# Sixteen consecutive pairs of experts summed by products, and row sums moved forward, in a hybrid decoder layer

## The chip, the cores and the metric

One Trainium2 chip, one core. The metric is the device time of one execution in microseconds (us), lower is better. The kernel is written by hand for each engine, with semaphores between them: TensorE (PE) for products, VectorE (DVE), ScalarE (ACT), GpSimd (POOL), and SyncE (SP), which issues the loads of weights.

## The reference, cut to what matters

One layer for 264 tokens (256 of a prompt, 8 samples), width 1024, all in float32. RWKV-7 time mixing and a convolution module are merged and projected, then comes the channel mixer, in which the change lies: 64 experts of width 256, of which each token takes 8 (out of 4 of 8 groups), and one shared expert.

```python
gate = jnp.sum(jax.nn.one_hot(eidx, N_EXPERTS) * wsel[..., None], axis=1)    # 8 of 64 per token
def expert_block(args):
    xb, gb = args
    h = silu(einsum('td,edf->tef', xb, w_gate)) * einsum('td,edf->tef', xb, w_up)
    h = h * gb[..., None]
    return einsum('tef,efd->td', h, w_down)
y = h + routed + shared        # then the final RMSNorm
```

Each expert has three matrices of 1 MB (w_gate, w_up, w_down), so the stage reads 192 MB of weights, in the order of the experts.

## The kernel before, in words

The first half of the run (to about 490 us) is the mixing part and the router. The change does not touch it.

In the experts' stage the experts are worked in 32 pairs, at places 0 to 31. Each expert has 64 slots, a pair fills the 128 rows of the array: two experts' matmuls run as halves (64 x 512). The weights stand in a ring of five slots (`NSLOT`), which SP refills when TensorE has finished with a slot (gate and up after `h_mm`, down after `yx_mm`), so weights are loaded about two and a half pairs ahead.

For a pair at place q TensorE does in this order, in the loop over q in `moe_pe`: `index(q+3)` (3 matmuls of one column that turn a one-hot tile into a list of token rows), `gate_up(q)` in two halves of 16 matmuls, between them `turn_hidden(q-1)` (2 transposes, L626), then `down(q-1)` (16 matmuls), and `turn(q+1)` (8 transposes of the next pair's token rows, L595). The token rows are gathered from `xg` by POOL (L1159). ACT makes the sigmoid, copies the turned tiles and stores half of the down product (`ye_act`); DVE multiplies the hidden tile (`hidden`, L981 and L982) and stores the other half (`take`, L990, `ye_dve`).

The pair's result `ye` (128 slots x 1024) comes to the tokens' sum `xrow` by one of two ways:

- **Stored pairs.** Four steps later POOL writes the rows that hold a token to `yrows` in DRAM with an indirect DMA (L1203). When all stored pairs are written, 24 gathers (`early_rows`, L1173: 3 tiles of tokens times their 8 experts, in order of tiles 0, 2, 1; tile 2 has 8 rows) bring rows back into a ring of five tiles (`NEB`), and DVE adds each one, weighted, with `add_early` (L1056). Rows of experts that were not stored are left out by the bounds check.
- **Product pairs** (`late(q)`). DVE makes a tile of gates (`late_gates`, L1017 to L1025) and TensorE turns it (`turn_gates`, 3 transposes, L660). Two places later TensorE multiplies it with `ye` (`combine(q)`, 4 small matmuls for the samples and 4 of 128 x 512) and DVE adds the product to `xrow` (`add_late`, L1035 and L1039). Nothing goes to DRAM.

Which pair is what is set by the tuple `LATE` (L337). Experts are renumbered over the places so that the stored pairs hold the lowest numbers (`PAIR`, `ROW_LIMIT`). `SUMS_FROM` and `SUMS` (L344) say how many of the 24 row sums are done by which place. In `pair(q)` on DVE half of a place's sums, rounded down, stand ahead of `hidden(q)`, the rest behind it, and `take(q-1)` behind those. At place 31 all stand ahead. On POOL, step i first fetches the token rows of pair i, then stores pair i-4, then issues the gathers of `rows_by(i)` to `rows_by(i+1)`: none before step `LAST_STORED + 4`, where it waits for all stores to land and issues five; after that as many in step i as the sums of place i-3. A gather waits for the sum that frees its tile. Step i starts after turn(i-2), which stands at the end of place i-3.

Of the kernel before, what the change touches and what calls it, by code (L numbers as in the profile page):

```python
# [111 lines left out]
def layer_step(nc, A, out, stop=9):  # L112

    ctx = ExitStack()
    with ctx:
# [218 lines left out]
        rowl = E.take(3, 8).bitcast(U32)  # L334
        E8 = x2T.rearrange("p k n -> p (k n)")[:, 0:8 * NE].rearrange("p (a e) -> p a e", a=8)
        NPAIR = NE // 2
        LATE = (14, 16, 18, 20, 24, 25, 26, 27, 28, 29, 30, 31)  # L337
        NLATE = len(LATE)
        FIRST = NPAIR - NLATE
        late = lambda q: q in LATE  # L340
        nlate = lambda q: sum(p < q for p in LATE)
        PAIR = [FIRST + nlate(q) if late(q) else q - nlate(q) for q in range(NPAIR)]
        LAST_STORED = max(q for q in range(NPAIR) if not late(q))
        SUMS_FROM, SUMS = 26, (0, 4, 8, 12, 16, 20, 24)  # L344
        sums_by = lambda q: SUMS[max(0, min(q - SUMS_FROM, len(SUMS) - 1))]
        NEB = 5
        xeT = [E.take(KT, 2 * SLOTS) for _ in range(2)]
# [1850 lines left out]
```

How the kernel before makes its waits and increments, by code:

```python
            def link(ins, name):  # L261
                note(ins, name)
                eng.wait_ge(S[name], cnt[name])
# [6 lines left out]
        def wait(eng, name, k):  # L270
            if k > 0:
                eng.wait_ge(S[name], k)
# [11 lines left out]
        def z_wait_free(eng, n):  # L284
            if n >= 2:
                kind = z_kind(n - 2)
                eng.wait_ge(S[f'z_free_{kind}'], sum(z_kind(m) == kind for m in range(n - 1)))
# [144 lines left out]
        def moe_sp(sp):  # L433
            for part, n in enumerate(('ws_gate', 'ws_up')):
                load_item(sp, part, SHARED_SLOT, A[n][0])
            for e in range(3):
                for part in range(3):
                    load_item(sp, part, e, expert_w(part, e))
            load_item(sp, 2, 3, expert_w(2, 3))
            sp.wait_ge(S['h2_ready'], 8)
            load_item(sp, 0, 4, expert_w(0, 4))
            sp.wait_ge(S['x2_ready'], 3)
            sp.dma_start(grow, A['normf_g'].rearrange("(a d) -> a d", a=1).partition_broadcast(128)) \
              .then_inc(S['grow_in'], 16)
            sp.dma_start(xg[0:NP, :].rearrange("(t p) d -> p t d", p=128), x2p[:, 0:2, :]).then_inc(S['x2_out'], 16)
            sp.dma_start(xg[NP:NT, :], x2p[0:NS, 2, :]).then_inc(S['x2_out'], 16)
            load_item(sp, 1, 4, expert_w(1, 4))
            sp.dma_start(wsd, A['ws_down'][0].rearrange("(j p) d -> p j d", p=128)).then_inc(S['wsd_in'], 16)
            sp.wait_ge(S['mk_ready'], 1)
            load_item(sp, 2, 4, expert_w(2, 4))
            sp.wait_ge(S['shg_mm'], 4)
```

## Time and profile before

| | us |
|---|---|
| median of 3 runs | 1061.78 |
| lowest, highest | 1061.06, 1062.14 |
| the profiled execution | 1062.62 |
| its span, first to last instruction | 1060.8 |
| TensorE busy | 955.1 (90%) |
| DVE busy | 526.3 (50%) |
| POOL busy | 330.0 (31%) |
| ACT busy | 233.7 (22%) |

The page divides the span into 40 slices of 26.5 us. TensorE's granted clock is given in tenths of full speed; a value of 1.00 is 2.4 GHz over the whole stretch, lower values are a mix with 1.2 GHz. In a timeline a number in brackets is the engine's idle time ahead of the row, and behind the arrow stands what ended it. A wait for several semaphores is put down to the one that came last. DMA's share is the mean busy share of 16 DMA engines.

### The profile page before, as it was taken

The numbers are of one execution on the slowest core, as the hardware profiler recorded it, in microseconds if no ns is written. First come the engines' busy times: TensorE is split into PE (matmuls) and PEld (weight loads), VectorE is DVE, ScalarE is ACT, GpSimd is POOL, SyncE is SP. The second block draws the span as 40 slices with busy tenths as digits, with TensorE's granted clock in tenths as the row PEclk, the third lists the DMA queues.
The fourth block names the chain that finished last, engine by engine and source line by source line (L and its number), as shares of the span: only waits on it lengthen the run. The fifth ranks groups of instructions, "written<-read, shape, count | busy, mean of one in ns | idle before, by whom it ended". The sixth has DMA issues, their size and how long they took to land.

```text
span 1060.8 us, 18129 instructions
## 1 busy us (share of the span) xinstructions
PE 955.1 (90%) x7399; PEld 572.7 (54%) x7399; DVE 526.3 (50%) x1053; ACT 233.7 (22%) x486; POOL 330.0 (31%) x363
## 2 busy tenths in 40 slices
PE   5999999999999988699998898879899998998995
PEld 4878877877787786348443333333333433333331
DVE  2158958875985778766232311111222321264665
ACT  3241134114312511433111111121111111111113
POOL 0049907951992498000011111010110101222310
PEclk9999999999999999899998999989999999999998
DMA  8635243525424265198799999999999999999961
GB/s 232 175 124 195 91 147 127 191 81 172 160 96 137 72 216 222 25 390 324 269 408 422 420 416 414 417 407 408 405 398 410 397 417 416 413 414 393 345 226 42
DMA packets 87502, 292.67 MB, mean 276 GB/s; under 512 B 17058, under 2 KB 48356, under 8 KB 62567
## 3 DMA queue, kind: packets, MB, share of 16 engines
q1 hardware_dynamic: 72647, 254.03, 62.2%
q0 software_dynamic: 14768, 37.43, 9.3%
q8 instruction: 61, 1.00, 0.4%
q14 instruction: 26, 0.21, 0.1%
HBM read 275.48 MB, written 33.16 MB: 291 GB/s over the span
## 4 chain that ended last, share of the span: by engine, by line
PE 64%; DMA 19%; DVE 7%; ACT 3%; SPq 3%; issue 2%; POOL 0%; DVEq 0%; POOLq 0%
PE bank L1358 62%; DMA big<-in_w_up 17%; ACT big L1655 3%; DMA big<-yrows,big 2%; DMA big<-in_w_in 1%; DVE big L1945 1%; SPq L400 1%; PE bank L595 1%; PE bank L626 1%; SPq L1311 1%; DVE big L1998 1%; DVE big L2002 0%; ACT L1655 0%; DVE big L1153 0%; SPq L1265 0%
## 5 line engine op out<-in xcount | busy, mean ns | idle before, releaser
L1358 PE MATMUL bank<-big 64*64 64x64 f32 (+8 forms) x6914 | 892.0, 358 | 84.8 <-DMA big<-in_w_up 35.5
L1358 PEld LDWEIGHTS bank<-big 64*64 64x64 f32 (+4 forms) x6914 | 517.5, 149 | 410.5 <-issue 316.3
L1655 ACT ACTIVATE big<-bank 128x512 f32<-128x512 f32 (+7 forms) x286 | 122.7, 452 | 663.6 <-PE bank L1358 388.7
L1159 POOL DMA_INDIRECT big<-xg,big x32 | 33.4, 1044 | 475.7 <-PE bank L595 374.3
L2149 POOL TENSOR_SCALAR big<-big 128x256 f32<-128x256 f32 x120 | 132.6, 1105 | 1.7
L981 DVE TENSOR_TENSOR big<-big,bank 128x256 f32<-128x256 f32 x32 | 13.5, 421 | 209.8 <-ACT big L1655 209.8
L2161 POOL TENSOR_TENSOR big<-big 128x256 f32<-128x256 f32 x120 | 94.2, 785 | 0.3
L1945 DVE SCALAR_TENSOR_TENSOR big<-big 128x256 f32<-128x256 f32 x120 | 79.6, 663 | 4.1
L1655 ACT ACTIVATE big<-big 128x272 f32<-128x272 f32 (+9 forms) x108 | 49.9, 505 | 43.6 <-DVE big L1880 11.3
L990 DVE COPY big<-bank 128x512 f32<-128x512 f32 x32 | 22.1, 689 | 57.2 <-PE bank L1358 57.2
L1655 ACT ACTIVATE big<-bank,big 128x272 f32<-128x272 f32 (+2 forms) x53 | 23.8, 475 | 111.9 <-PE bank L1358 111.9
L2145 POOL TENSOR_SCALAR big<-big 128x256 f32<-128x256 f32 x4 | 2.2, 550 | 148.3 <-DVE big L1923 148.3
L595 PEld LDWEIGHTS bank<-big 128*128 128x128 f32 x256 | 27.4, 141 | 25.2 <-issue 25.2
L1039 DVE TENSOR_TENSOR big<-big,bank 128x512 f32<-128x512 f32 x48 | 33.0, 689 | 14.4 <-PE bank L1358 14.4
L1655 ACT ACT_TABLE_LOAD x30 | 38.5, 1283 | 3.2 <-DVE big L899 2.0
L1173 POOL DMA_INDIRECT big<-yrows,big x24 | 26.0, 1081 | 37.1 <-DVE big L1056 19.2
L1862 DVE SCALAR_TENSOR_TENSOR big<-bank,big 128x272 f32<-128x272 f32 x26 | 12.9, 496 | 45.4 <-ACT big L1655 45.4
L595 PE MATMUL bank<-big 128*128 128x128 f32 x256 | 35.0, 280 | 0.0
L1056 DVE SCALAR_TENSOR_TENSOR big<-big 128x1024 f32<-128x1024 f32 (+1 forms) x24 | 30.7, 1278 | 7.3 <-DMA big<-yrows,big 6.2
L1025 DVE COPY big<-bank 128x264 f32<-128x264 f32 x12 | 5.2, 433 | 42.5 <-PE bank L660 42.5
L626 PEld LDWEIGHTS bank<-big 128*128 128x128 f32 x64 | 10.1, 205 | 26.0 <-issue 26.0
L1203 POOL DMA_INDIRECT yrows<-big x20 | 21.4, 1070 | 6.1 <-issue 6.1
(164 smaller groups left out, 441.3 us busy)
## 6 DMA issues: line engine op xcount, KB each, us to landing
big<-in_w_gate SPq DMA_DIRECT2D x64, 1024.0 KB, 15.5
big<-in_w_up SPq DMA_DIRECT2D x64, 1024.0 KB, 21.0
big<-in_w_down SPq DMA_DIRECT2D x64, 1024.0 KB, 14.1
big<-in_w_in SPq DMA_DIRECT2D x29, 1024.0 KB, 5.2
yrows<-big POOLq DMA_DIRECT2D x32, 512.0 KB, 3.3
big<-in_w_out SPq DMA_DIRECT2D x2, 2048.0 KB, 14.8
big<-in_state_wkv SPq DMA_DIRECT2D x32, 64.0 KB, 2.3
out_wkv_s<-big SPq DMA_DIRECT2D x32, 64.0 KB, 3.7
```

The source lines that it names most:

```text
L595: ins = nc.tensor.transpose(ps_x[h][:, 128 * (k % 4):128 * (k % 4) + 128], xe[q % NXE][:, 128 * k:128 * k + 128], ident)
L990: note(v.tensor_copy(ye[q % NYE][:, 512:1024], ps_y[1][:, :]), 'ye_dve')
L1039: note(v.tensor_tensor(x, x, comb_bank(q, n), AD), 'cb_sum')
L1056: note(v.scalar_tensor_tensor(out=xrow[0:r, t, :], in0=early[k % NEB][0:r, :], scalar=gate8a[0:r, t, j:j + 1], in1=xrow[0:r, t, :], op0=M, ...
L1159: pool.indirect_dma_start(out=x[0:n, :], out_offset=None, in_=xg, in_offset=bass.IndirectOffsetOnAxis(ap=idxu[0:n, col:col + 1], axis=0), ...
L1173: pool.indirect_dma_start(out=early[k % NEB][0:r, :], out_offset=None, in_=yrows[0:PASS, :], in_offset=bass.IndirectOffsetOnAxis(ap=rowu[0 ...
L1203: pool.indirect_dma_start(out=yrows[0:PASS, :], out_offset=bass.IndirectOffsetOnAxis(ap=rowsu[:, c:c + 1], axis=0), in_=ye[q % NYE], in_of ...
L1358: return nc.tensor.matmul(out_, lhsT=lhsT, rhs=rhs, start=start, stop=stop)
L1655: return nc.scalar.activation(out_, in_, f, **kw)
L1945: note(v.scalar_tensor_tensor(out=acc, in0=u, scalar=cw, in1=acc, op0=M, op1=AD), 'tap')
L2149: note(gp.tensor_scalar(TP[:, w % 3, :], u, cw, None, ALU.mult), 'tapm')
L2161: note(gp.tensor_tensor(acc, acc, TP[:, w % 3, :], ALU.add), 'tapm')
```

## The change

Sixteen pairs, at places 16 to 31, are product pairs in place of twelve (14, 16, 18, 20 and 24 to 31). With that the places 14 and 15 are both stored, and 17, 19, 21, 22, 23 are no longer. The last stored pair is 15 in place of 23, so POOL's wait for the stores and its first five gathers stand in step 19 in place of 27. The row sums are spread three to a place over places 19 to 26, in place of four to a place over 26 to 31. `PAIR` becomes the identity, `ROW_LIMIT` goes from 2560 to 2048 rows.

```diff
-        LATE = (14, 16, 18, 20, 24, 25, 26, 27, 28, 29, 30, 31)
+        LATE = tuple(range(16, 32))
...
-        SUMS_FROM, SUMS = 26, (0, 4, 8, 12, 16, 20, 24)
+        SUMS_FROM, SUMS = 19, (0, 3, 6, 9, 12, 15, 18, 21, 24)
```

On TensorE, place 19 before: index of 22 (bank0, 128x1), the two halves of the gate and up products (bank4) around turn_hidden (bank5), down (bank6, bank7) and turn (bank1, bank2).

```order
L1358 MATMUL bank0<-big 128x1 x3
L1358 MATMUL bank4<-big 64x512 x8
L626 MATMUL bank5<-big 128x128 x2
L1358 MATMUL bank4<-big 64x512 x8
L1358 MATMUL bank6<-big 64x512 x4
L1358 MATMUL bank7<-big 64x512 x4
L595 MATMUL bank1<-big 128x128 x4
L595 MATMUL bank2<-big 128x128 x4
```

The same place in the changed kernel, up to the down products.

```order
L1358 MATMUL bank0<-big 8x256 x4
L1358 MATMUL bank1<-big 128x512
L1358 MATMUL bank2<-big 128x512
L1358 MATMUL bank1<-big 128x512
L1358 MATMUL bank2<-big 128x512
L1358 MATMUL bank0<-big 128x1 x3
L1358 MATMUL bank4<-big 64x512 x8
L626 MATMUL bank5<-big 128x128 x2
L660 MATMUL bank0<-big 128x128 x2
L660 MATMUL bank0<-big 128x8
L1358 MATMUL bank4<-big 64x512 x8
```

The combine of pair 17 (the first five rows) and the gate transposes of pair 19 (L660) have come in. A row of x8 stands for 16 matmuls of the trace where each is issued in two parts.

On POOL, the end of the stage before: from the store of pair 23 (the second row) on. L1159 fetches token rows, L1203 stores, L1173 is a gather for a row sum.

```order
L1159 DMA big<-xg,big 128x1024
L1203 DMA yrows<-big 4096x1024
L1173 DMA big<-yrows,big 128x1024 x5
L1159 DMA big<-xg,big 128x1024 x2
L1173 DMA big<-yrows,big 128x1024 x3
L1173 DMA big<-yrows,big 8x1024
L1159 DMA big<-xg,big 128x1024
L1173 DMA big<-yrows,big 8x1024 x4
L1159 DMA big<-xg,big 128x1024
L1173 DMA big<-yrows,big 8x1024 x3
L1173 DMA big<-yrows,big 128x1024 x8
```

And of the changed kernel, from the store of pair 15 in step 19 on, up to step 28.

```order
L1203 DMA yrows<-big 4096x1024
L1173 DMA big<-yrows,big 128x1024 x5
L1159 DMA big<-xg,big 128x1024 x3
L1173 DMA big<-yrows,big 128x1024 x3
L1159 DMA big<-xg,big 128x1024
L1173 DMA big<-yrows,big 8x1024 x3
L1159 DMA big<-xg,big 128x1024
L1173 DMA big<-yrows,big 8x1024 x3
L1159 DMA big<-xg,big 128x1024
L1173 DMA big<-yrows,big 8x1024 x2
L1173 DMA big<-yrows,big 128x1024
L1159 DMA big<-xg,big 128x1024
```

The gathers have moved eight steps forward, and a step now issues three of them, each group behind the fetch of a pair's token rows.

## Rows read from the trace of the kernel before

**Rows 1.** The page's 40 slices: busy tenths, clock, DMA and GB/s.

```profile
PE   5999999999999988699998898879899998998995
PEclk9999999999999999899998999989999999999998
DMA  8635243525424265198799999999999999999961
GB/s 232 175 124 195 91 147 127 191 81 172 160 96 137 72 216 222 25 390 324 269 408 422 420 416 414 417 407 408 405 398 410 397 417 416 413 414 393 345 226 42
```

**Rows 2.** Chain that ended last, by time: start us, us, what.

```profile
692.95 19.17 DMA big<-in_w_up
...
888.96 20.43 DMA big<-in_w_up
...
946.91 16.62 DMA big<-yrows,big
...
1003.51 8.03 PE bank L1358 x32
```

**Rows 3.** Timeline of TensorE, places 14 to 28: start us, us, operation, idle before.

```profile
729.03 5.35 PE L1358 MATMUL bank<-big 128*64 128x512 f32 x16 [2.03 <-DMA big<-in_w_up]
...
734.65 0.54 PE L660 MATMUL bank<-big 128*128 128x128 f32 x3
...
742.14 1.09 PE L595 MATMUL bank<-big 128*128 128x128 f32 x8
...
745.86 5.35 PE L1358 MATMUL bank<-big 128*64 128x512 f32 x16 [1.98 <-DMA big<-in_w_up]
...
811.63 5.35 PE L1358 MATMUL bank<-big 128*64 128x512 f32 x16 [1.60 <-DMA big<-in_w_up]
...
943.13 8.67 PE L1358 MATMUL bank<-big 128*8 128x256 f32 x38 [0.94 <-ACT big L1655]
```

**Rows 4.** Windows: places 16-17, 17, 18-23, 24-27, 27, 28, 29.

```profile
core 0: us, PE busy (x) PEld busy (x) DVE busy (x) ACT busy (x) POOL busy (x), PEclk, DMA share, GB/s
758.59:789.82 31.23, 30.31 (x150) 12.30 (x148) 9.47 (x22) 4.86 (x10) 3.03 (x3) 1.00 0.98 399
776.95:789.82 12.87, 12.78 (x67) 5.24 (x65) 2.44 (x7) 2.43 (x5) 2.02 (x2) 1.00 0.96 383
789.82:887.54 97.72, 92.24 (x441) 37.47 (x439) 26.93 (x63) 14.58 (x30) 9.09 (x9) 0.98 1.00 410
887.54:959.56 72.02, 64.75 (x303) 26.60 (x301) 29.21 (x56) 9.72 (x20) 14.92 (x15) 0.95 1.01 415
941.10:959.56 18.46, 17.52 (x86) 7.06 (x84) 9.89 (x18) 2.43 (x5) 4.89 (x5) 1.00 1.02 413
959.56:983.66 24.10, 18.95 (x85) 7.51 (x83) 13.42 (x20) 2.43 (x5) 5.33 (x5) 0.93 0.92 362
983.66:1001.48 17.82, 16.89 (x80) 6.18 (x78) 11.00 (x16) 2.43 (x5) 7.50 (x8) 1.00 0.95 355
```

**Rows 5.** Timeline of DVE, places 26 to 31, row sums and takes.

```profile
941.58 0.68 DVE L990 COPY big<-bank 128x512 f32<-128x512 f32 x1
...
955.98 1.28 DVE L1056 SCALAR_TENSOR_TENSOR big<-big 128x1024 f32<-128x1024 f32 x1 [1.71 <-DMA big<-yrows,big]
...
963.55 1.28 DVE L1056 SCALAR_TENSOR_TENSOR big<-big 128x1024 f32<-128x1024 f32 x1 [2.45 <-DMA big<-yrows,big]
964.76 0.68 DVE L990 COPY big<-bank 128x512 f32<-128x512 f32 x1
...
1035.91 0.68 DVE L990 COPY big<-bank 128x512 f32<-128x512 f32 x1
1037.81 0.42 DVE L981 TENSOR_TENSOR big<-big,bank 128x256 f32<-128x256 f32 x1 [1.22 <-ACT big L1655]
```

**Rows 6.** Timeline of POOL: first gather of its 27th step, next fetch, next gathers.

```profile
922.80 1.02 POOL L1173 DMA_INDIRECT big<-yrows,big  x1 [12.12 <-DMA yrows<-big]
...
929.30 0.99 POOL L1159 DMA_INDIRECT big<-xg,big  x1 [0.30 <-issue]
...
944.32 0.99 POOL L1173 DMA_INDIRECT big<-yrows,big  x1 [0.30 <-issue]
```

## The prediction, made before the changed kernel had run

> **What bounds the kernel now.** I read first the page's 40 slices, to find the stage that the change touches: from about 500 us on, the experts' stage, DMA is busy nine tenths or more and moves 400 GB/s and more until slice 37 [rows 1]. The page's TensorE digit is also 8 or 9 there, so the averages don't say which of the two sets the pace. The chain of waits does, by place in the order of pairs: where a pair is stored the chain goes through the landing of w_up, and it goes through TensorE's matmuls alone in the last pairs; between them stands one piece of 16.62 us on a gather from yrows [rows 2].
>
> The TensorE timeline gives the period of each pair, if one takes the start of turn (L595 x8) as a pair's end. Two things are to be seen in it [rows 3]. At places 14, 15 and 19 TensorE waits 1.6 to 2.0 us for w_up, and then its first 16 matmuls of gate and up take 5.35 us. At a product pair the x38 row (combine, index and the same 16) starts after 0.94 us of idle on ACT's release and needs 8.67 us, with no wait for DMA behind it.
>
> The windows turn that into prices [rows 4]. Place 17, a pair without combine that didn't wait, took 12.87 us. Place 27, with index, combine and gate transposes, took 18.46 us, of which TensorE was busy 17.52 us at a granted clock of 1.00 (2.4 GHz). Place 29, which has no index, took 17.82 us. So a combine with the gate transposes and the idle around it costs TensorE 5.6 us. DMA's pace lies between: from the w_up-bound start at 745.86 (place 15) to that at 811.63 (place 19) are 65.77 us for four pairs, 16.44 us a pair [rows 3]. A stored pair is under the DMA's pace by 3.6 us, a product pair is over it by 2.0 us. **Before, the two kinds alternate from 14 to 20 and a product pair's excess is paid out of its neighbour's slack. That is what the change takes away.**
>
> **The change part by part.** The order of instructions says it does what its table says: at place 19 TensorE now has a combine and gate transposes, and POOL starts its gathers four places after store 15 rather than after store 23. Everything below is measured against the profiled execution (span 1060.8 us, its own time 1062.62 us; the median of the runs, 1061.78 us, is 0.84 us less).
>
> Places 0 to 15: nothing. The experts' order there differs only at 14 and 15. Place 14 loses its three gate transposes (0.54 us) behind a wait for w_up of 1.98 us at place 15 [rows 3], which covers them; that cover would not have to be there for a loss, only for the absence of a gain. Place 14 gains a store. 264 tokens times 8 rows of 4 KB are 2112 rows over 32 pairs, so 66 rows or 0.27 MB a pair: 0.66 us at the 410 GB/s of the stage [rows 4], and it is issued in place 16.
>
> Places 16 and 17: they lose the combine of 14, since 14 and 15 are now stored, so nothing covers the wait for w_up. Before they took 31.23 us at clock 1.00 without a DMA wait [rows 4]. Now the DMA's pace decides: place 17's gate products start two periods after 745.86, at 778.7, and from such a start to the next turn are 13.11 us (729.03 to 742.14, with gate transposes) [rows 3]. End of 17 at 791.8 instead of 789.82: **+2.0 us**. Bounds: 0 if the weights are ahead, +3.3 with both extra stores in front of them.
>
> Places 18 to 23: six pairs with index, combine and gate transposes, 6 x 18.46 = 110.8 us. Before these six took 97.72 us, three of them without a combine [rows 4]: **+13.0 us**. Is TensorE really the bound there? From 18 to 26 the DMA must move 9 x (6 weights of 1.05 MB and 0.27 MB of token rows) = 59.0 MB, and the 24 gathers, half of the 2112 rows, 4.3 MB: 63.3 MB, at 410 GB/s 154 us against 9 x 18.46 = 166 us. It has 12 us over, and the sums' load is not even: three full gathers together are 1.6 MB, 3.8 us, less than the 2 us a pair that have been gathered up by then plus the ring's lead. The sum has no DMA wait in it.
>
> A rule of the Trainium skill speaks against this kernel at this point: DMA: Bandwidth & Descriptors, Specifications, gives a core about 358 GB/s of HBM. By that the 63.3 MB would need 177 us, an estimate from that page, and the sum would be 11 us more. This trace differs: 410 and 415 GB/s over 97.72 and 72.02 us [rows 4], and the measurement decides.
>
> Places 24 to 27: 4 x 18.46 = 73.84 us against 72.02 us; the old stretch had two DMA waits but also one pair without combine [rows 4]: **+1.8 us**.
>
> Place 28: it took 24.10 us, 5.64 us more than its work [rows 4]. The vector engine's rows say why: the row sums (L1056) of the place ahead waited again and again for a gather, the last ended at 964.8, and only then came take (L990), on which the combine of 26, at the head of place 28, waits [rows 5]. The gathers were issued from 944.32 on, three us into the pair that needed them, and three of its four sums fed on them [rows 6]. The change makes the sums three a pair, so only the last of the three feeds on a gather issued at the end of the pair before; the other two have been out a pair longer. Place 28 itself has no sums left. 24.10 becomes 18.46: **-5.6 us**. Could the stall only move? In place 27 the first gather, issued at 944.32, let its sum start at 955.98, 14.9 us into the pair; two sums behind the hidden products are harmless if they end by 18.9 us into the pair, as they did in place 26, where take ran from 941.58 and the x38 row still started on ACT's release [rows 3, 5]. The third sum starts at about 17.6, so 2.7 us are left at the three places (20, 25, 26) where its gather is a large one. I take nothing for it; the ends are 0 and the whole 5.6 us again.
>
> Place 29 to the end: the four row sums of place 31 go, but take of 30 there waited for nothing that they held: hidden of 31 started at 1037.81 on ACT's release, 1.22 us after take had ended, so they lay in cover [rows 5]. **0 us.** The vector engine's own load is no bound: 9.89 to 13.42 us in pairs of 18.46 and more [rows 4]. POOL at its 19th step waits for store 15 and then issues five gathers. Before that was 12.12 us of idle and 6.4 us of issue, and the next token gather stood behind it [rows 6]; its pair is turned more than a pair later, so it costs nothing. If that cover failed, turn would wait.
>
> Sum: 2.0 + 13.0 + 1.8 - 5.6 = **+11.2 us**, 1073.8 us for a run like the profiled one and **1073.0 us** beside the median. The clock is in these rows: all prices of product pairs are at 1.00. The x16 row's 5.35 us after each DMA wait would vanish with the waits, and this is inside the 18.46.
>
> **The rivals.** (A) The gather stall stays, at one of places 20, 25, 26, or at several: the DMA queue stays full and the third gather lands later than 17.6 us into its pair. For it: one landed 16.62 us after issue [rows 2]. Against it: that was the last of four with full rows; its price is 2 to 5.6 us, 1075 to 1078.6 us, and more at two places.
>
> (B) The DMA doesn't recover. Place 29 moved only 355 GB/s with a busy share of 0.95 [rows 4]. If mixing products and loads held the DMA to that, 63.3 MB need 178 us, 12 us over TensorE's 166: about 1085 us. Against it: place 27 did the same work at 413 GB/s.
>
> (C) Faster: the DMA is the bound all the way and its bytes decide. Four stores and an eighth of the gathers' rows go, 2 x 264 rows of 4 KB = 2.2 MB, 5.3 us at 410 GB/s, and the stall of 5.6 us too: 1062.62 - 10.9 = 1051.7 us. It decides if a product pair can run below 16.4 us. The row of place 27 with 17.52 us of TensorE's busy time at full clock speaks against it.
>
> (D) No change: places 16 to 23 lose, but the end gains the same, because the waits of 24, 25 and 28 and the x16 rows at low clock held more than I count: 1060 to 1064 us. The prices above leave no room for it.
>
> **How the numbers follow.** A measurement of this kernel can tell about 0.2%, 2.1 us, from no change. My forecast, +8 to +14 us, has 0.78; A 0.11; B 0.05; C 0.03; D 0.03. The range takes in the forecast's bounds below (no loss at 16 and 17, some waits shorter: -3 us) and A's one stall above: 1070 to 1079 us. B, C and D and the upper part of A are left out. Faster 0.03, same 0.03, slower 0.94.
>
> **What would show it.** In the profile after: turn-to-turn periods of 18.46 us from place 18 to 28, no wait for w_up behind place 17, and the GB/s digits down to about 355 to 390 from slice 30 on. Place 16 starts its gate products on w_up, near 762. Row sums start near place 19 and none is left after place 26; DVE waits for yrows come to under 3 us in all. The chain runs from place 18 to the end in TensorE. I am wrong if waits for w_up come back after 18 (B), if take ends late behind a sum (A), or if product pairs run below 18 us (C).

## The result, and the profile after

The changed kernel takes 1076.52 us (median of 4 runs, 1073.83 to 1077.90), the kernel before 1061.42 us in the same comparison. The ratio is 1.0144 with a 95% interval of 1.012 to 1.0167: slower by 1.4%, some 15 us. The forecast was 1073.0 us, in a range of 1070 to 1079.

The profiled execution took 1077.1 us, its span is 1074.7 us, 13.9 us more than before. The page of the changed kernel, its slices:

```profile
PE   5999999999999987799989889888899999999995
PEclk9999999999999999899999899989899999999997
DMA  8645253425524275296899999999999999998911
GB/s 229 174 128 196 80 169 120 168 81 169 186 103 124 67 252 177 93 421 235 335 419 419 404 420 417 415 414 410 386 412 412 416 363 379 382 399 343 380 63 42
```

Beside [rows 1], TensorE's digit is 9 from slice 30 to 39 without a break, and the GB/s fall to 343 to 399 in slices 33 to 38; before, slices 33 to 36 had 413 to 417. The queue is no longer what the last part of the stage waits for.

The windows, cut at the starts of turn (the transposes of the next pair's token rows, L595): places 16 and 17, 18 to 23, 24 to 27, 28, 29 and 30, and the end from turn(31) on.

```profile
core 0: us, PE busy (x) PEld busy (x) DVE busy (x) ACT busy (x) POOL busy (x), PEclk, DMA share, GB/s
757.10:789.80 32.70, 29.17 (x136) 12.11 (x135) 7.91 (x20) 4.86 (x10) 4.08 (x4) 0.90 0.97 387
789.80:900.46 110.66, 105.15 (x500) 42.35 (x499) 59.58 (x105) 14.57 (x30) 22.32 (x23) 1.00 0.99 400
900.46:974.31 73.85, 70.11 (x335) 28.25 (x333) 39.30 (x70) 9.72 (x20) 10.89 (x11) 1.00 0.95 384
974.31:992.77 18.46, 17.52 (x86) 7.05 (x84) 6.56 (x14) 2.43 (x5) 0.98 (x1) 1.00 0.89 356
992.77:1028.40 35.63, 33.76 (x156) 12.35 (x155) 12.34 (x22) 4.86 (x10) 0.99 (x1) 1.00 0.77 307
1028.40:1074.70 46.30, 32.42 (x129) 11.49 (x127) 19.10 (x32) 11.06 (x22) 0.00 (x0) 0.86 0.13 47
```

The stage can be added up against [rows 4]:

| stretch | before, us | after, us | difference | forecast |
|---|---|---|---|---|
| up to the end of place 15 | 758.59 | 757.10 | -1.5 | 0 |
| places 16 and 17 | 31.23 | 32.70 | +1.5 | +2.0 |
| 18 to 23 | 97.72 | 110.66 | +12.9 | +13.0 |
| 24 to 27 | 72.02 | 73.85 | +1.8 | +1.8 |
| 28 | 24.10 | 18.46 | -5.6 | -5.6 |
| 29 and 30 | 35.64 | 35.63 | 0 | 0 |
| from turn(31) to the end | 41.50 | 46.30 | +4.8 | 0 |
| sum | 1060.8 | 1074.7 | +13.9 | +11.2 |

(35.64 is 1019.30, the start of turn(31) before, less 983.66, the end of place 28.) From places 16 and 17 down to 29 and 30 the table is within 0.5 us of the forecast. The first line is not, and the last is off by 4.8 us. The timeline of TensorE in the changed kernel, first at places 16, 17 and 18, then at the end:

```profile
762.15 6.52 PE L1358 MATMUL bank<-big 128*64 128x512 f32 x16 [3.31 <-DMA big<-in_w_up]
...
778.39 3.65 PE L1358 MATMUL bank<-big 128*64 128x512 f32 x16 [0.22 <-DMA big<-in_w_up]
...
791.72 8.68 PE L1358 MATMUL bank<-big 128*8 128x256 f32 x38 [0.83 <-ACT big L1655]
...
1051.54 3.65 PE L1358 MATMUL bank<-big 128*64 128x512 f32 x16 [0.47 <-ACT big L1655]
1058.95 7.14 PE L1358 MATMUL bank<-big 128*8 128x256 f32 x16 [3.76 <-issue]
```

The waits for w_up end with place 17, as forecast. From there to place 30 TensorE has no gap but the 0.9 us ahead of each combine. The last row is the combine of pair 31. The kernel before has this row at the same point:

```profile
1047.18 4.26 PE L1358 MATMUL bank<-big 128*8 128x256 f32 x16 [1.10 <-DVE big L990]
```

Before, it starts 0.35 us after the vector engine's copy and needs 4.26 us. Now it starts 3.0 us after that copy, released by nothing that the profile's waits show, and needs 7.14 us. Over these matmuls the granted clock is 0.59, most of them at half the clock, as their window shows:

```profile
1058.90:1066.20 7.30, 7.14 (x16) 2.48 (x16) 3.49 (x6) 3.25 (x7) 0.00 (x0) 0.59 0.00 0
```

The chain of waits of the changed kernel has the stall as a piece of its own:

```profile
1051.54 3.68 PE bank L1358 x16
1055.21 0.02 issue
1055.24 0.70 DVE big L990
1055.94 3.02 issue
1058.95 4.77 PE bank L1358 x12
1063.72 0.02 issue
1063.75 0.69 DVE big L1039
```

What stands between the two matmul rows in TensorE's program is a branch: `with pe.If(count > SLOTS)`, the overflow pass for experts with more than 64 tokens, which isn't taken with these inputs, so TensorE jumps over its code to `combine(NPAIR - 1)`. The experiments begin there.

### The profile page after: what moved, and what is told of

Its sections match the earlier page's. It is cut to its first block, busy times and chain, and to the rows that moved or that the text cites. A ratio compares the mean times of both kernels' runs of the same rounds, so it can differ in the third digit from the quotient of the medians.

```text
span 1074.7 us, 18349 instructions
## 1 busy us (share of the span) xinstructions
PE 972.3 (90%) x7475; PEld 577.7 (54%) x7475; DVE 543.8 (51%) x1085; ACT 233.7 (22%) x486; POOL 323.0 (30%) x359
## 3 DMA queue, kind: packets, MB, share of 16 engines
q8 instruction: 62, 1.02, 0.4%
## 4 chain that ended last, share of the span: by engine, by line
PE 70%; DMA 14%; DVE 7%; ACT 4%; SPq 3%; issue 2%; DVEq 0%
PE bank L1358 67%; DMA big<-in_w_up 13%; ACT big L1655 3%; DMA big<-in_w_in 1%; DVE big L1945 1%; PE bank L595 1%; PE bank L626 1%; SPq L400 1%; SPq L1311 1%; DVE big L1998 1%; PE bank L660 0%; DVE big L2002 0%; ACT L1655 0%; DVE big L1153 0%; SPq L1265 0%
## 5 line engine op out<-in xcount | busy, mean ns | idle before, releaser
L1358 PE MATMUL bank<-big 64*64 64x64 f32 (+10 forms) x6978 | 907.1, 359 | 82.7 <-DMA big<-in_w_up 31.3
L1358 PEld LDWEIGHTS bank<-big 64*64 64x64 f32 (+4 forms) x6978 | 521.1, 149 | 419.8 <-issue 320.2
L1159 POOL DMA_INDIRECT big<-xg,big x32 | 33.3, 1042 | 476.7 <-PE bank L595 399.6
L1039 DVE TENSOR_TENSOR big<-big,bank 128x512 f32<-128x512 f32 x64 | 44.0, 689 | 19.4 <-PE bank L1358 19.4
L595 PEld LDWEIGHTS bank<-big 128*128 128x128 f32 x256 | 27.4, 141 | 25.2 <-issue 25.2
L1862 DVE SCALAR_TENSOR_TENSOR big<-bank,big 128x272 f32<-128x272 f32 x26 | 12.9, 496 | 45.8 <-ACT big L1655 45.8
L595 PE MATMUL bank<-big 128*128 128x128 f32 x256 | 35.0, 280 | 0.0
L1173 POOL DMA_INDIRECT big<-yrows,big x24 | 23.2, 968 | 19.3 <-DMA yrows<-big 12.3
L1035 DVE TENSOR_TENSOR big<-big,bank 104x256 f32<-104x256 f32 x16 | 6.7, 421 | 30.2 <-PE bank L1358 30.2
```

The source lines that it names most:

```text
L595: ins = nc.tensor.transpose(ps_x[h][:, 128 * (k % 4):128 * (k % 4) + 128], xe[q % NXE][:, 128 * k:128 * k + 128], ident)
L1039: note(v.tensor_tensor(x, x, comb_bank(q, n), AD), 'cb_sum')
L1159: pool.indirect_dma_start(out=x[0:n, :], out_offset=None, in_=xg, in_offset=bass.IndirectOffsetOnAxis(ap=idxu[0:n, col:col + 1], axis=0), ...
L1173: pool.indirect_dma_start(out=early[k % NEB][0:r, :], out_offset=None, in_=yrows[0:PASS, :], in_offset=bass.IndirectOffsetOnAxis(ap=rowu[0 ...
L1358: return nc.tensor.matmul(out_, lhsT=lhsT, rhs=rhs, start=start, stop=stop)
```

## The experiments

All times are medians against the kernel before on the same chip; "the end" is the stretch from turn(31) on, 41.50 us in the kernel before.

**1 and 2. The branch taken out, of both kernels.** These two leave out TensorE's part of the overflow pass.

```diff
-            with pe.If(count > SLOTS):
-                for c in range(1, MAXPASS):
...
             combine(NPAIR - 1)
```

> The changed kernel with TensorE's branch around the overflow pass taken out (the branch and what it skips; it isn't executed with these inputs, so the pass is left out on TensorE alone). Theory 1 (code behind a taken branch): the 3.76 us in which TensorE stood before the combine of pair 31, released by nothing, and the low clock after it (7.14 us for 16 matmuls instead of 4.26) are the branch. Both go: the span from turn(31) to the end falls from 46.3 to 41 us or less, the time by 4.5 to 6 us. Theory 2 (the stretch depends on who is late there, the row sums having gone from place 31): the 46.3 us stay within 0.5 us.

Measured: 1072.19 us, 4.3 us below the changed kernel (5.4 between the profiled executions), ratio to the kernel before 1.0119 (1.0083 to 1.0155). This interval overlaps with the changed kernel's (1.012 to 1.0167), so the times alone don't settle it; the place of the difference in the trace does. The timeline of TensorE in this kernel, and the window of the end:

```profile
1051.49 3.65 PE L1324 MATMUL bank<-big 128*64 128x512 f32 x16 [0.47 <-ACT big L1621]
1056.25 4.26 PE L1324 MATMUL bank<-big 128*8 128x256 f32 x16 [1.10 <-DVE big L956]
```

```profile
1028.36:1069.80 41.44, 29.54 (x129) 10.58 (x127) 19.11 (x32) 11.07 (x22) 0.00 (x0) 0.93 0.14 52
```

The end is 41.44 us again. The stall and the low clock behind it are both gone, and the 18.46 us of each place are as they were (turn(19) at 808.14, turn(29) at 992.74 us).

> The same cut in the kernel before. Theory 1: the 1.10 us idle before the combine of 31 become about 0.3 to 0.4 after the vector engine's copy, or about 0.8 less; time lower by 0 to 1.5 us, much less than for the changed kernel. Theory 2: the same, no difference. If this falls by as much as the changed kernel does, the branch costs both the same and the 4.8 us are something else.

Measured: 1061.78 us, ratio 1.0009 (0.9989 to 1.0029), with 1.10 us of idle and 4.26 us of combine as with the branch. The expectation had room for a small gain; there is none. So the branch costs nothing in the profile of the kernel before and 4.8 us in that of the changed kernel. Its mere presence isn't the cause.

**3 to 5. The code moved.** Matmuls of one column made twice, at places 3 to 15, where TensorE waits for weights. They write the same values again and make the program longer: 13 lists of three matmuls, 78 matmul records. The diff is that of pad_before.

```diff
+                if 6 <= q <= 18:
+                    lists(2 * SLOTS, q % NIX, OH[q % 2])
                 note(lists(2 * SLOTS, q % NIX, OH[q % 2]), 'idx_mm')
```

> The kernel before with 13 lists of three one-column matmuls made twice (places 3 to 15), 78 matmul records more, about as many as the four combines of the change add (76), all in places where TensorE waits for the DMA. Theory 1 in its narrow form (what counts is how far the branch stands in TensorE's program): the end from turn(31) on goes from 41.5 to about 46.3 us, the time up by 4 to 5 us, with the rest unchanged. Theory 2, or a stall of the branch that doesn't hang on the position: the end stays at 41.5 us, time within 1 us of before.

Measured: 1064.28 us, ratio 1.0042 (1.0022 to 1.0062), 3.7 us over the kernel before where 4 to 5 were expected. The timeline of TensorE:

```profile
1042.41 0.61 PE L1360 MATMUL bank<-big 128*8 128x256 f32 x6 [1.10 <-DVE big L992]
1044.50 5.76 PE L1360 MATMUL bank<-big 128*8 128x256 f32 x10 [1.48 <-issue]
```

The kernel before now has a stall too, at another point: six matmul records of the combine run, then TensorE stands for 1.48 us with nothing to release it, and the other ten take 5.76 us. From the start of the combine to the end of the span are 17.2 us (1042.41 to 1059.6) instead of 13.6, and the end is 45.1 us, where 46.3 were expected.

The same on the changed kernel, with 7 and with 14 lists:

> The changed kernel with 7 lists of three one-column matmuls made twice at places 3 to 15 (42 matmul records), in the shadow of the waits for w_up there. Theory 1 (the stall at the branch hangs on where the code behind it stands): the 3.76 us of idle before the combine of 31 change, to 1.10 us or to a piece that cuts the combine, while the 18.46 us of places 18 to 28 stay. If they stay at 3.0 to 3.8 us with a low clock behind them, position within a hundred instructions isn't what counts.

> The same with 14 lists (84 records). Theory 1: again another stall than the changed kernel's, and the three together (0, 42, 84 records more) differ by 2 us or more in the end from turn(31) on. Rival: all three within 1 us of 46.3 us.

Measured, one execution each: 1074.66 and 1073.40 us, and the row of the combine is in both what it was before the change. With 14 lists:

```profile
1057.98 4.26 PE L1361 MATMUL bank<-big 128*8 128x256 f32 x16 [1.10 <-DVE big L993]
```

The end is 41.4 us in both. One execution each says little in time, since the changed kernel's own go from 1073.83 to 1077.90 us, but the row is plain: 42 matmul records more in the program remove the stall. All kernels with the branch, by the length of TensorE's program:

| kernel | matmul records more than before | idle at the combine of 31, us | its matmuls, us |
|---|---|---|---|
| before, sums_before, sums2_before | 0 | 1.10 | 4.25 to 4.26 |
| alt13 | 19 | 1.10 | 4.26 |
| alt14, run14, alt14_s3 | 38 | 1.10 to 1.17 | 4.26 |
| changed kernel | 76 | 3.76 | 7.14 |
| late_only | 76 | 3.56 | 5.95 |
| pad_before | 78 | 1.10, then 1.48 | 0.61 and 5.76 |
| pad_after7 | 118 | 1.10 | 4.26 |
| pad_after14 | 160 | 1.10 | 4.26 |

The alt kernels, run14, the sums kernels and late_only are described further down. The stall comes at 76 to 78 records more and at no other length tried, also in late_only, which has the changed kernel's program on TensorE and other row sums. Its cause is the length of the code ahead, not what the engines did. The Trainium skill has a mechanism for it (Runtime: NRT & Kernel Launch, Instruction fetch mechanics): a sequencer streams its instructions in blocks of 16 KiB, one after another, and a taken branch whose target isn't in the window forces a fetch of the target's block.

The traces show such fetches. The page lists an instruction queue with 61 packets and 1.00 MB before, 16.4 KB each; without TensorE's branch and the code that it skips there are 59, and 60 in place of the changed kernel's 62. The DMA view of 8 us around the combine, in 40 slices of 0.2 us, where 82 GB/s in one slice are one such packet: the changed kernel from 1052, the kernel before from 1043, pad_before from 1038.

```profile
GB/s 0 0 0 82 0 0 0 0 0 0 0 0 0 0 0 0 0 0 0 0 82 0 41 0 0 0 0 0 0 0 0 0 0 0 0 0 0 0 0 0
```

```profile
GB/s 0 0 82 0 0 0 0 0 0 0 0 0 0 0 0 0 0 0 0 82 0 0 0 0 0 0 0 0 0 0 0 0 0 0 0 0 0 0 0 0
```

```profile
GB/s 0 0 0 82 0 0 0 0 0 0 0 0 0 0 0 0 0 0 0 0 82 0 0 0 0 0 0 0 0 0 0 0 0 0 0 0 0 0 0 0
```

Each has two packets 3.4 us apart (the 41 belongs to another, smaller queue). In the changed kernel the second starts near 1056.1 and TensorE goes on at 1058.95, 2.8 us later. In pad_before it starts near 1042.1 and TensorE goes on in mid-combine at 1044.50, 2.4 us later; in late_only near 1062.1 and at 1064.45, 2.3 us later. In the kernel before it starts near 1046.9, and the combine runs from 1047.18 without a break. This fits one reading: the first packet brings the branch's target, the second the code behind it, and TensorE stands only where it runs off the first block before the second is in. Which instructions a packet holds no trace shows, and no padded kernel was run without the branch.

**6 and 7. Product pairs: how many, or where?** Both have fourteen of them and move the same bytes, with the same row sums (3, 3, 4, 5, 5, 4 a place). New against the kernel before are 12 and 22 in alt14, 17 and 19 in run14.

```diff
+        LATE = (12, 14, 16, 18, 20, 22, 24, 25, 26, 27, 28, 29, 30, 31)        # alt14
+        LATE = (14, 16, 17, 18, 19, 20, 24, 25, 26, 27, 28, 29, 30, 31)        # run14
+        SUMS_FROM, SUMS = 26, (0, 3, 6, 10, 15, 20, 24)
```

> Fourteen product pairs, the two new ones (12 and 22) with a stored pair on either side, and row sums at 3, 3, 4, 5, 5, 4 from place 26 on. Theory P (a product pair costs only where its neighbour is one too: 18.46 us of TensorE against a DMA pace of 16.4, and 12.87 for a stored pair): the two cost nothing, and 0.54 MB of stores and as much of gathers go, 2.6 us. So 0 to 3 us faster than the kernel before with the same row sums (sums2_before). Rival N (each product pair costs its 5 us of TensorE, wherever it stands): 4 to 10 us slower than sums2_before.

> Also fourteen product pairs and the same row sums as alt14, with the same number of stores and gathered rows, but the new ones are 17 and 19, so that 16 to 20 are five in a row. Theory P: places 17 and 19 take 18.46 us each instead of 12.9 and 16.1; of these 8 us some come back at 21 to 23, where TensorE waited 3 to 4 us for w_up. So 3 to 7 us slower than alt14 and sums2_before. Rival N: the same as alt14 within 1 us.

Measured: alt14 1054.99 us, ratio 0.9953 (0.9937 to 0.9968); run14 1065.94 us, ratio 1.0040 (1.0023 to 1.0058). Where the two new pairs stand makes 11 us, more than the 3 to 7 expected. Theory P holds, with sizes larger than expected, and rival N (no difference) falls. Against sums2_before (1058.88 us) alt14 is 3.9 us faster and run14 7.1 us slower. Places 16 to 20 and 21 to 23 of run14:

```profile
757.98:845.17 87.19, 83.25 (x401) 33.96 (x399) 32.05 (x70) 12.15 (x25) 6.02 (x6) 1.00 0.96 394
845.17:894.22 49.05, 47.09 (x227) 18.71 (x225) 13.58 (x31) 7.29 (x15) 3.99 (x4) 1.00 0.90 361
```

In and behind the run of five the DMA falls back to 394 and 361 GB/s. A fair comparison must hold the same work. A pair's combine stands two places behind it, so the stretch is places 14 to 26, in which each kernel has seven combines; run14, then alt14:

```profile
723.80:947.18 223.38, 205.96 (x973) 83.74 (x971) 69.89 (x156) 31.59 (x65) 24.09 (x24) 0.97 0.97 395
```

```profile
723.57:936.20 212.63, 201.28 (x970) 82.26 (x968) 68.45 (x153) 31.59 (x65) 24.24 (x24) 0.99 1.00 407
```

Both start it at the same time, and run14 ends it 11.0 us later, of which 10.8 are its own. alt14 takes 16.4 us a place, the DMA's pace of the prediction, with the queue full all the way. run14 lets the queue fall back in places 16 to 23 and has to wait for weights afterwards: place 25 starts its products after 3.64 us of idle on w_up and takes 19.6 us, and the DMA is at 417 GB/s over places 25 and 26. What TensorE won back at places 23 and 24 (12.87 and 13.87 us) it paid again at 25 and 26 (19.56 and 19.53); the expectation had seen only the first half of this. The spans differ by 12.5 us; the other 1.5 are in the end.

**8 to 10. The row sums.**

> The changed kernel's sixteen product pairs with the old row sums (26 to 31, four a place). The stores have landed long before; the first five gathers are issued at step 19, the others from place 26 on, one pair before use, as in the kernel before. Theory S with the DMA's load as its cause: from place 18 on TensorE is the bound and the queue is no longer full, so gathers land in under 10 us and place 28 has no stall; the time is that of the changed kernel within 1.5 us (1074 to 1078, if the branch costs the same). Theory S with the freshness alone as its cause: the stall of place 28 is back, 3 to 5.6 us over the changed kernel.

Measured: 1080.85 us, ratio 1.0194 (1.0167 to 1.0220), 4.3 us over the changed kernel's median, which is from another comparison; 4.7 between the profiled spans. Places 27 and 28:

```profile
954.84:973.30 18.46, 17.52 (x85) 7.06 (x84) 9.90 (x18) 2.43 (x5) 4.90 (x5) 1.00 0.94 377
973.30:998.38 25.08, 18.97 (x85) 7.54 (x83) 13.42 (x20) 2.43 (x5) 5.16 (x5) 0.86 0.77 306
```

and the vector engine in them:

```profile
969.55 1.29 DVE L1056 SCALAR_TENSOR_TENSOR big<-big 128x1024 f32<-128x1024 f32 x1 [1.53 <-DMA big<-yrows,big]
...
974.55 1.29 DVE L1056 SCALAR_TENSOR_TENSOR big<-big 128x1024 f32<-128x1024 f32 x1 [2.93 <-DMA big<-yrows,big]
...
978.26 1.29 DVE L1056 SCALAR_TENSOR_TENSOR big<-big 128x1024 f32<-128x1024 f32 x1 [2.42 <-DMA big<-yrows,big]
979.47 0.68 DVE L990 COPY big<-bank 128x512 f32<-128x512 f32 x1
```

The stall is back in full, 6.6 us instead of 5.6, though the DMA now runs at 377 GB/s in place 27 (busy share 0.94) instead of 413 (1.02). The three fresh gathers, issued at 958.40, 959.70 and 961.00, let their sums start 11.2, 14.9 and 17.3 us later; in the kernel before it was 11.7, 14.2 and 16.6 us. What counts is that a sum's gather is issued in the place that needs it; a queue that is a tenth less loaded didn't make it faster. How a gather fares beside an idle queue was not run. Without its new row sums the change would have cost 4 to 5 us more.

The other side, the kernel before with gentler row sums:

```diff
-        SUMS_FROM, SUMS = 26, (0, 4, 8, 12, 16, 20, 24)
+        SUMS_FROM, SUMS = 26, (0, 3, 6, 10, 14, 19, 24)        # sums_before
+        SUMS_FROM, SUMS = 26, (0, 3, 6, 10, 15, 20, 24)        # sums2_before
```

> The kernel before with its row sums at 3, 3, 4, 4, 5, 5 a place from 26 on, instead of six times 4. Theory S (the stall of 5.6 us in place 28 is the fresh gathers: three of four sums of place 27 feed on gathers issued in that place): the sums of place 27 feed on the first five gathers, place 28 takes 18.5 us instead of 24.1, and the time falls by 4 to 6 us, to about 1056. Rival (the queue is full and the wait moves to place 28 or 29, or to the five sums of place 31): a wait of 2 us or more for yrows there, and the time falls by less than 3 us.

> The kernel before, row sums at 3, 3, 4, 5, 5, 4 a place. The earlier spread with five sums ahead in place 31 lost 1.9 us there (take was late by 1 us, combine after it by as much). Theory S: with four in place 31 the end from turn(31) on is 41.5 us again, place 28 stays near 18.5 to 19.5, and the time is 4 to 6 us under the kernel before. Rival: the five fresh gathers of place 30 are late and take 1 to 3 us back.

Measured: 1057.86 us, ratio 0.9987 (0.9970 to 1.0004), and 1058.88 us, ratio 0.9984 (0.9969 to 0.9998). The stall is gone in both (place 28 takes 19.5 and 18.5 us), but the gain is about half of the 4 to 6 us that I expected, and in sums_before under the 3 us that the expectation gave to its rival. Part is given back where five sums stand in one place, as sums2_before's timeline of TensorE shows at the head of places 30 and 31:

```profile
998.52 8.03 PE L1358 MATMUL bank<-big 128*8 128x256 f32 x32 [1.78 <-DVE big L990]
...
1017.25 8.03 PE L1358 MATMUL bank<-big 128*8 128x256 f32 x32 [1.85 <-DVE big L990]
```

The idle time is 0.94 with four sums; each place with five costs 0.85 to 0.9 us. In sums_before the five of place 30 and the five ahead of take in place 31 made the end 43.4 us (1011.27 to 1054.7), 1.9 us more. In place 26, the first with row sums, TensorE takes 18.46 us as before, so their effect starts at turn(27). From there on the profiles are 2.7 and 3.9 us shorter (117.0 and 115.8 us against 119.7); the medians fell by 2.7 and 2.4. The profiled spans fell by 6.1 and 4.1 us, but what goes beyond lies ahead of that point and is scatter.

**11 and 12. Attempts at better.**

> alt14 with row sums at 3, 4, 4, 4, 5, 4. Five sums in a place made TensorE wait 0.85 us more for take at the head of places 30 and 31; here only one place has five. Theory S: 0.8 us less there, but place 27 has two fresh gathers of four sums instead of one of three, whose second may come 1 us late: the time within 1 us of alt14. Rival (freshness decides): place 28 gets a stall of 2 us or more.

Measured: 1056.34 us, ratio 0.9942 (0.9922 to 0.9962), not to be told from alt14. One of the two waits of 1.8 us for take is left, and places 27 and 28 are 18.46 us each: two fresh gathers of four sums are still harmless.

> One more stored pair in the alternation (25, with 24 a product pair), so the run of product pairs is 26 to 31; the first gathers can't be issued before step 29 and 24 row sums must fit in places 28 to 31 (5, 6, 7, 6). Theory P alone: place 25 and 26 take the DMA's pace instead of 18.46, 3 to 4 us less than alt14. Theory S: six sums a place with a ring of five tiles wait for gathers of 10 us and more, 4 to 12 us lost at places 29 to 31. I expect S to win: 2 to 8 us slower than alt14.

Measured: 1069.90 us, ratio 1.0080 (1.0054 to 1.0107), 15 us over alt14, nearly twice what I had expected at most. TensorE waits five times for take at places 29 to 31, 17.4 us in all (the last of them the 1.10 us that every kernel without the stall has); the three longest:

```profile
976.52 9.68 PE L1358 MATMUL bank<-big 128*8 128x256 f32 x32 [4.28 <-DVE big L990]
...
1001.18 9.45 PE L1358 MATMUL bank<-big 128*8 128x256 f32 x32 [6.13 <-DVE big L990]
...
1022.97 8.03 PE L1358 MATMUL bank<-big 128*8 128x256 f32 x32 [3.49 <-DVE big L990]
```

Six and seven sums a place don't fit beside the pair's own work with a ring of five tiles.

alt14 beats both kernels: 0.47% (0.32 to 0.63%) under the kernel before. It has more product pairs than that and fewer than the changed one, and none of the new ones next to another.

## Why the prediction was right, and where it wasn't

- **The bound changes at place 18, and a product pair is 18.46 us.** Right to 0.1 us over ten places: 110.66 for six, 73.85 for four. Run14 against alt14 shows the mechanism apart from the number of pairs. The working says that 24 to 27 had one pair without combine before; there were two, 24 and 25, since a combine stands two places behind its pair. The 72.02 us are measured, so the sum isn't touched.
- **Places 16 and 17.** Forecast +2.0, measured +1.5. The wait for w_up at place 16 came as said, at 762.15 us. At place 17 it was only 0.22 us, at 778.39 us where 778.7 was worked out. Place 17 ended at 789.80 us, not at 791.8: the gain ahead of place 16 hides in the +1.5.
- **Nothing ahead of place 16.** The profile has -1.5 us there. The places are the same but for gate transposes and one store, and noif_after reached the same point at 756.11 us. So did noif_before, with the old order, at 755.75 us. I take it for scatter: of 25 executions of the kernel before in one comparison the times go from 1054.9 to 1063.1 us.
- **The stall of place 28.** Right in size and in cause. late_only brings it back, sums_before removes it from the kernel before. Its size is that of one profile: in noif_before, which has the same row sums, places 27 and 28 take 23.11 and 21.13 us, 7.3 us over two of 18.46. Rival A thought of a full queue; the stall came at 377 GB/s as well. The third sum of a place started 17.7 us into it (at 825.9 in the place from 808.15 on), as worked out, and no sum in the changed kernel waited for yrows at all. The gathers began as said, behind 12.3 us of POOL's wait for the stores, which cost nothing.
- **Place 29 to the end, 0 us.** This is the term that was wrong: +4.8 us. I had looked at the work in place 31 (row sums, take, hidden) and found it in cover, and that holds: from turn(31) to the products of L1358 behind the last turn_hidden are 23.14 us, 23.13 before. The step that failed is that equal work takes equal time: the four new combines move the code behind TensorE's branch, and there it meets a stall of 2.7 us (3.02 in the chain against 0.35) and a combine that at the lower clock holds the chain for 4.77 instead of 2.55 us. With the term at +4.8 the sum would have been 16.0 against 13.9 in the profile and about 15 in the medians.
- **The range.** That 1076.52 us lies in it owes something to luck. The upper end, 1079, was there for rival A's stall, which didn't come; the branch, of which the prediction knows nothing, filled that room.
- **The signs.** The chain runs through TensorE from place 18 on, as said. The GB/s didn't fall from slice 30 on but from slice 33 (412 to 416 in slices 30 to 32).
- **Rivals.** B (the DMA doesn't recover) fell: in place 26, with gathers under way, the DMA moved 413 GB/s at a period of 18.47 us, and place 28 took 18.46 us at 356. The 358 GB/s limit of the Trainium skill (DMA: Bandwidth & Descriptors, Specifications) would have made it 177 us for places 18 to 26; they took 166.1 us (789.80 to 955.85), at 400 GB/s over the first six. C and D fell with the 18.46 us.

## What to carry to other kernels

When work is moved from the DMA to an engine, count it against the slack of its own neighbours: two resources that alternate over a buffer of two or three steps share their slack only over that distance. Here the same number of moved pieces cost 11 us more in a row than spread out. Issue a gather at least one step before the one that uses it. And where a program jumps over code near its end, a change of length ahead of it can cost some us on the critical path (3 to 5 here), so a difference of that size has to be located in the trace before it is explained by the work.

## What the runs showed of the hardware

The branch: idle time of 1.10, 3.56 to 3.76, or 1.10 and then 1.48 us at the same combine, by the length of the program ahead of it, and the stall ends 2.3 to 2.8 us after the start of a 16.4 KB packet of the instruction queue. Behind the stall the granted clock was 0.59 over the combine of the changed kernel, which then took 2.9 us more (1.7 in late_only). Over the end the clock was 0.86 in the changed kernel, 0.93 without the branch, and 0.92 in the kernel before. In places 18 to 28, at 95% busy with a gap of 0.94 us in each, the granted clock stayed at 1.00 throughout. The weights and gathers of places 18 to 23 moved at 400 GB/s, those of alt14's places 14 to 26 at 407 GB/s. Row sums on tiles of 8 rows took 1.26 us each, as those of 128 rows did at 1.28.
